# Decay and key mask accumulated by TensorE in two attentions of a two-layer kernel, and the forgetting attention one unit apart

## The reference, cut to what matters

```python
# sparse attention: of the keys of a query only the selected ones count
_, sel = lax.top_k(score, topk)
logits = jnp.einsum('bthd,btkhd->bhtk', qblk, k_sel) * scale
logits = logits - slopes * dist
p = jax.nn.softmax(jnp.where(sel_ok, logits, -inf))

# forgetting attention: a decay, cumulated over the tokens, is added to the logits
log_f = jax.nn.log_sigmoid(f_logit)
cum_f = jnp.cumsum(log_f, axis=1)
logits = jnp.einsum('bhqd,bhkd->bhqk', qb, kb) * scale
logits = logits + cum_f[..., qs:qe, None] - cum_f[..., None, :qe]
p = jax.nn.softmax(jnp.where(causal, logits, NEG_INF))

# pooling mixer: moving means of four widths, less the input, times a 64x64 matrix for each group
groups.append((cs_g - lagged) / count - uf)
y = einsum('bsgc,gcd->bsgd', p, w_pool) * pool_scale
```

## Time and profile before

| what | value |
|---|---|
| median of three runs | 3217.14 us |
| the profiled execution's own time | 3217.12 us |
| its span, first to last instruction | 3215.0 us |
| mean granted clock of TensorE, share of 2.4 GHz | 0.961 |
| busy: TensorE, VectorE, ScalarE, GpSimd | 3027.6, 1371.4, 643.4, 1456.7 us |
| chain that ended last: TensorE, VectorE, DMA, ScalarE | 86%, 4%, 3%, 2% of the span |

### The profile page before, as it was taken

The page is one execution under the profiler, slowest core; times in us unless marked ns, Lnnn a source line. Parts: engine busy times, 40 slices in busy tenths (PEclk is TensorE's granted clock), DMA queues, the critical chain, the costliest instruction groups (busy, mean ns, idle before and its releaser), DMA issues.

```text
span 3215.0 us, 33121 instructions
## 1 busy us (share of the span) xinstructions
PE 3027.6 (94%) x13405; PEld 2224.9 (69%) x13405; DVE 1371.4 (43%) x2007; ACT 643.4 (20%) x1068; POOL 1456.7 (45%) x895
## 2 busy tenths in 40 slices
PE   7999979789999999999999787999998999999997
PEld 4444446457888888887886444667666888887886
DVE  0499957646523235343307334111312532335323
ACT  1401046421100001210302443110121211121111
POOL 2000100345665657666665112335435666667663
PEclk8999989889999999999999778999999999999998
DMA  4111136132333333433432000333333233333332
GB/s 96 33 40 33 39 102 176 53 113 85 96 108 92 104 93 95 129 92 92 120 97 66 1 1 7 79 102 108 79 91 132 86 98 95 91 103 116 95 100 64
DMA packets 364920, 273.23 MB, mean 85 GB/s; under 512 B 14048, under 2 KB 334816, under 8 KB 364768
## 3 DMA queue, kind: packets, MB, share of 16 engines
q1 hardware_dynamic: 357568, 253.30, 27.6%
q10 hardware_dynamic: 4720, 10.68, 0.9%
q0 software_dynamic: 2480, 7.13, 0.7%
HBM read 262.59 MB, written 8.49 MB: 84 GB/s over the span
## 4 chain that ended last, share of the span: by engine, by line
PE 86%; DVE 4%; DMA 3%; issue 3%; ACT 2%; POOL 2%; SPq 0%; DVEq 0%; ACTq 0%; POOLq 0%
PE PS L803 38%; PE PS L815 24%; PE PS L755 5%; PE PS L769 4%; DMA ring<-in_w_in 3%; PE PS L446 3%; PE PS L459 2%; PE PS L1023 2%; PE PS L479 2%; PE PS L875 2%; PE PS L970 1%; POOL w_low L1888 1%; PE PS L471 1%; PE PS L889 1%; ACT arena L519 1%
## 5 line engine op out<-in xcount | busy, mean ns | idle before, releaser
L1888 POOL TENSOR_TENSOR w_low<-ring,w_high 128x1024 fp32r<-128x1024 f32 x382 | 940.9, 2463 | 31.9
L1885 POOL TENSOR_SCALAR w_high<-ring 128x1024 fp32r<-128x1024 f32 x382 | 427.1, 1118 | 865.9 <-PE PS L815 372.4
L815 PE MATMUL PS<-w_high,hid_high 128*128 128x512 f32 x864 | 337.2, 390 | 9.1 <-issue 9.1
L815 PE MATMUL PS<-w_high,hid_low 128*128 128x512 f32 x864 | 336.8, 390 | 0.0
L815 PE MATMUL PS<-w_low,hid_high 128*128 128x512 f32 x864 | 336.7, 390 | 0.0
L1947 POOL TENSOR_TENSOR arena<-arena 128x896 f32<-128x896 f32 (+5 forms) x24 | 39.8, 1677 | 582.0 <-DVE arena L1484 358.5
L803 PE MATMUL PS<-hT_high,w_high 128*128 128x512 f32 x656 | 272.2, 415 | 15.1 <-POOL w_low L1888 15.1
L803 PE MATMUL PS<-x1T_high,w_high 128*128 128x512 f32 x704 | 275.0, 391 | 3.5 <-DVE x1T_low L1587 3.5
L803 PE MATMUL PS<-x1T_high,w_low 128*128 128x512 f32 x704 | 274.6, 390 | 0.0
L803 PE MATMUL PS<-x1T_low,w_high 128*128 128x512 f32 x704 | 274.4, 390 | 0.0
L803 PE MATMUL PS<-hT_high,w_low 128*128 128x512 f32 x656 | 256.9, 392 | 0.0
(11 more groups left out here) (265 smaller groups left out, 4901.3 us busy)
## 6 DMA issues: line engine op xcount, KB each, us to landing
ring<-in_w_ff SPq DMA_DIRECT2D x128, 512.0 KB, 3.8
ring<-in_w_in SPq DMA_DIRECT2D x112, 512.0 KB, 3.9
ring<-in_w_gu SPq DMA_DIRECT2D x88, 512.0 KB, 3.8
ring<-in_w_ada SPq DMA_DIRECT2D x48, 512.0 KB, 5.1
ring<-in_w_down SPq DMA_DIRECT2D x44, 512.0 KB, 3.6
ring<-in_w_out SPq DMA_DIRECT2D x32, 512.0 KB, 4.5
ring<-in_w_branch SPq DMA_DIRECT2D x16, 512.0 KB, 3.9
arena<-in_x SPq DMA_DIRECT2D x8, 512.0 KB, 6.9
```

Of the source, the lines that this page charges most:

```text
L815: mm = pe.matmul(PS[:, 2 * p + half, :], x[:, k, at], w[:, q, half_of(half)], start=(first and n == 0), stop=(last and n == 2))
L1885: pool.tensor_scalar(w_high[:, q, :], ring[:, s, :], 1.0, 1.0, ALU.mult, ALU.mult).then_inc(weights_high, 1)
L1888: pool.tensor_tensor(w_low[:, q, :], ring[:, s, :], w_high[:, q, :].bitcast(F32), ALU.subtract).then_inc(weights_used[s], 1)
```

## The change

It adds an argument more to Attention: a second matmul accumulated on each score product. For the sparse attention that is a bf16 identity times the key mask, on all 128 partitions, for b of at least 2; GpSimd's adds and their buffers go. For the forgetting attention it is a selector holding -8 in the row of its head, times cum_r, which holds the cumulated decay as a rounded high part in rows 0 to 7 and 64 to 71 and the rest in rows 32 to 39 and 96 to 103, both in fp32r, K = 64 on the same half as the scores. The spreads, their copies and GpSimd's causal adds go; one causal row serves all units as bias. ScalarE makes the high parts and VectorE the low ones. All three attentions now have lag 1 written in; the forgetting one gets six buffers and the sparse one's order of units. The pool product becomes a fill of its first four units in bank 7, scaled beside them by VectorE.

```diff
-        cbias = view(141.5, 4, S)
+        ident16 = view(142, P // 2).bitcast(BF16)
...
-        selw = view(28, 8, P)
+        selw, selw_r = view(24, 8, P), rounded("selw_r", 28, 8, P)
+        cum_r = rounded("cum_r", 24, S)
+        causal_row = view(20, S)
         qk2T = view(96, 8, S)
         z2T = view(128, 8, S)
-        negcum = [view(152, 2, S), view(136, 2, S)]
-        prob2 = [view(kb, S) for kb in (160, 164, 168, 172)]
-        probT2 = [view(176, NB, 2 * P), view(20, NB, 2 * P)]
+        prob2 = [view(kb, S) for kb in (160, 164, 168, 172, 152, 156)]
+        probT2 = [view(176, NB, 2 * P), view(136, NB, 2 * P)]
...
-                return 2 * (u % (2 + self.lag)) + m
+                return 2 * (u % 3) + m
...
+                            more = self.more(pe, u, m, c, w) if self.more is not None else None
                             mm = pe.matmul(PS[:, 2 * m + c // 512, 0:w], self.q(j, m, b), self.k(j, m, c, w),
-                                           start=True, stop=True)
+                                           start=True, stop=more is None)
+                            if more is not None:
+                                mm = pe.matmul(PS[:, 2 * m + c // 512, 0:w], *more, start=False, stop=True)
...
-                for u in range(last + 1 + self.lag):
+                for u in range(last + 2):
                     if u < last:
                         scores(u + 1)
                     if self.fill is not None and u <= last:
                         self.fill(pe, u)
-                    t = u - self.lag
+                    t = u - 1
                     if t >= 1 and self.closes(t - 1):
...
-                    if u >= 2 + self.lag:
-                        dve.wait_ge(self.turned, self.turns_before[u - 1 - self.lag])
+                    if u >= 3:
+                        dve.wait_ge(self.turned, self.turns_before[u - 2])
...
-        pairs4 = [(j, b) for j in range(4) for b in reversed(range(NB))]
+        pairs4 = [(j, b) for j in range(4) for b in (6, 7, 0, 1, 4, 5, 2, 3)]
...
+            return bias8[:, 2 * j + m, P * (NB - 1 - b):S], None, 0
+
+        def c_mask(pe, u, m, c, w):
+
+            _, b = pairs2[u]
             if b < 2:
-                return bias8[:, 2 * j + m, P * (NB - 1 - b):S], None, 0
-            k = selected.index(u)
-            return cbias[:, 2 * (k % 2) + m, 0:P * (b + 1)], cbias_made, 2 * k + m + 1
+                return None
+            pe.wait_ge(ident16_made, 1)
+            return ident16, mask[b][:, c:c + w]
 
         def f_bias(u, m):
-            j, b = pairs4[u]
-            return negcum[j % 2][:, m, 0:P * (b + 1)], fbias_made, 2 * u + m + 1
+            _, b = pairs4[u]
+            return causal_row[:, P * (NB - 1 - b):S], causal_row_made, 1
+
+        def f_decay(pe, u, m, c, w):
+
+            j, _ = pairs4[u]
+            if u == 0:
+                pe.wait_ge(cum_split, 2)
+            r = slice(64 * m, 64 * m + 64)
+            return selw_r[r, 2 * j + m, :], cum_r[r, c:c + w]
...
-        SPREAD_AT = {4: (0, 0), 3: (0, 1), 2: (1, 0), 1: (1, 1)}
-
-        def spread_fill(pe, u):
-
-            j, b = pairs4[u]
-            if j == 3 or b not in SPREAD_AT:
+        def pool_fill(pe, u):
+
+            if u >= 4:
                 return
-            m, half = SPREAD_AT[b]
-            n = 4 * j + 4 - b
-            if n:
-                pe.wait_ge(negcum_made, n)
-            pe.matmul(PS[:, 7, :], selw[0:8, 2 * (j + 1) + m, :], fl[0:8, half * 512:(half + 1) * 512],
-                      start=True, stop=True).then_inc(spread_done, 1)
-
-        def spread_after(act, u):
-            j, b = pairs4[u]
-            if j == 3 or b not in SPREAD_AT:
-                return
-            m, half = SPREAD_AT[b]
-            act.wait_ge(spread_done, 4 * j + 4 - b + 1)
-            act.activation(negcum[(j + 1) % 2][:, m, half * 512:(half + 1) * 512], PS[:, 7, :], ACT.Copy, scale=-8.0
-                           ).then_inc(negcum_made, 1)
+            g, half = divmod(u, 2)
+            if u == 0:
+                pe.wait_ge(pool_w_loaded, 64)
+            else:
+                pe.wait_ge(br_bc_made, 2 + u)
+            pe.wait_ge(pooled, g + 1)
+            pe.matmul(PS[:, 7, :], pool_w[:, g, :], z2T[:, g, 512 * half:512 * half + 512], start=True, stop=True
+                      ).then_inc(pool_mixed, 1)
...
-            prob, [probT_c[:, m] for m in range(2)], (4, 5), 1, fill_c, after_c)
+            prob, [probT_c[:, m] for m in range(2)], (4, 5), fill_c, after_c, c_mask)
...
-            prob2, probT2, (4, 5), 0, spread_fill, spread_after)
+            prob2, probT2, (4, 5), pool_fill, None, f_decay)
...
-            pe.wait_ge(cum_done, 1)
-            pe.wait_ge(selw_made, 1)
-            for m in range(2):
-                p = L.pair("spread_cum", 0, m)
-                pair_here(pe, "spread_cum", 0, m)
-                for half in HALVES:
-                    mm = pe.matmul(PS[:, 2 * p + half, :], selw[0:8, m, :], fl[0:8, half_of(half)], start=True, stop=True)
-                mm.then_inc(psum_full[p], 1)
-            pe.wait_ge(pool_w_loaded, 64)
-            for g in range(2):
-                p = L.pair("pool", 0, g)
-                pe.wait_ge(pooled, g + 1)
-                pair_here(pe, "pool", 0, g)
-                for half in HALVES:
-                    mm = pe.matmul(PS[:, 2 * p + half, :], pool_w[:, g, :], z2T[:, g, half_of(half)], start=True, stop=True)
-                mm.then_inc(psum_full[p], 1)
             all_pairs_free(pe, "branch")
             forget.pe(pe)
             pe.wait_ge(forget.out_stored, forget.n_out)
-            pe.wait_ge(br_bc_made, 4)
+            pe.wait_ge(br_bc_made, 6)
...
-            act.wait_ge(br_bc_made, 2)
-            for m in range(2):
-                p = L.pair("spread_cum", 0, m)
-                unit_here(act, "spread_cum", 0, m)
-                act.activation(negcum[0][:, m, :], flat(p), ACT.Copy, scale=-8.0).then_inc(psum_free[p], 1)
-            act.wait_ge(br_bc_made, 4)
+            act.wait_ge(cum_done, 1)
+            for r in (slice(0, 8), slice(64, 72)):
+                act.copy(cum_r[r, :], fl[0:8, :]).then_inc(cum_high, 1)
             forget.act(act)
...
+            dve.wait_ge(selw_made, 5)
...
-            dve.tensor_tensor_scan(fl[0:8, :], lsf_b[0:8, :], lsf_a[0:8, :], 0.0, ALU.mult, ALU.add
-                                   ).then_inc(cum_done, 1)
+            do(dve.tensor_tensor_scan(fl[0:8, :], lsf_b[0:8, :], lsf_a[0:8, :], 0.0, ALU.mult, ALU.add))
+            dve.memset(cum_r[:, :].bitcast(F32), 0.0).then_inc(cum_done, 1)
+
+            dve.wait_ge(cum_high, 2)
+            for r in (slice(32, 40), slice(96, 104)):
+                dve.tensor_tensor(cum_r[r, :], fl[0:8, :], cum_r[0:8, :].bitcast(F32), ALU.subtract
+                                  ).then_inc(cum_split, 1)
...
-                unit_here(dve, "pool", 0, g)
-                dve.tensor_scalar(z2T[:, g, :], flat(p), pscale[:, g:g + 1], None, ALU.mult).then_inc(psum_free[p], 1)
-                freed(dve, "pool", 0, g)
-                dve.sem_inc(br_bc_made, 1)
-            forget.dve(dve, link)
+
+            def pool_out(u):
+                if u < 4:
+                    g, half = divmod(u, 2)
+                    dve.wait_ge(pool_mixed, u + 1)
+                    dve.tensor_scalar(z2T[:, g, half_of(half)], PS[:, 7, :], pscale[:, g:g + 1], None, ALU.mult
+                                      ).then_inc(br_bc_made, 1)
+
+            forget.dve(dve, link, pool_out)
...
-            for k, u in enumerate(selected):
-                j, b = pairs2[u]
-                for m in range(2):
-                    if k >= 2:
-                        pool.wait_ge(sparse.logits_made, 2 * selected[k - 2] + m + 1)
-                    pool.tensor_tensor(cbias[:, 2 * (k % 2) + m, 0:P * (b + 1)],
-                                       bias8[:, 2 * j + m, P * (NB - 1 - b):S], mask[b], ALU.add
-                                       ).then_inc(cbias_made, 1)
+            pool.tensor_copy(ident16, ident[:, :]).then_inc(ident16_made, 1)
...
-                    do(pool.memset(selw[0:8, :, :], 1.0))
-                    pool.affine_select(out=selw[0:8, :, :], in_=selw[0:8, :, :], compare_op=ALU.is_equal, fill=0.0,
-                                       base=0, pattern=[[-1, 8], [0, P]], channel_multiplier=1).then_inc(selw_made, 1)
+                    do(pool.memset(selw, -8.0))
+                    for r in (slice(32 * q, 32 * q + 32) for q in range(4)):
+                        pool.affine_select(out=selw[r], in_=selw[r], compare_op=ALU.is_equal, fill=0.0,
+                                           base=0, pattern=[[-1, 8], [0, P]], channel_multiplier=1).then_inc(selw_made, 1)
+                    pool.wait_ge(selw_made, 4)
+                    pool.tensor_copy(selw_r[:, :, :], selw).then_inc(selw_made, 1)
...
-            for u, (j, b) in enumerate(pairs4):
-                for m in range(2):
```

(11 more changed lines are left out.)

34 lines of the change are left out of this document (14 added, 20 removed).

## The result

| | before | after |
|---|---|---|
| median of 4 runs each, us | 3216.05 (3208.64 to 3218.6) | 3196.96 (3195.87 to 3201.94) |
| profiled execution, us (its span) | 3217.12 (3215.0) | 3197.6 (3195.9) |
| mean granted clock of TensorE | 0.96 | 0.97 |

The ratio of the medians is 0.9949, with a 95% interval of 0.9935 to 0.9962: 19 us less, where 23 less were forecast. The stages show where it lies. The times are VectorE's, from the start of its first logits to the end of its last store in each stage, read from the timelines of the two profiles.

The account below looks back on a forecast made before the run. No engine was taken to bound the forgetting stage, only a loop of waits per unit. Terms -38 (that stage), +10 (its start), +5 (sparse stage), 0 (selector weights) made -23 us: 3194 us, own range 3178 to 3208, 80% range 3160 to 3222.

Parts of the forecast that it names:

- the side that had 0.77: Whole kernel: faster by over 0.3%, that is below 3207.5 us, given a chance of 0.77.
- The sparse stage: Mask products and lost overlap of the heads' scores on TensorE, less relief from GpSimd's adds: +5 us, ends -10 and +26.
- I put 60% on the path: Sparse stage: of TensorE's middle extra of 26 us, 60% lengthens the stage, 15.6 us; the rest hides where VectorE was full.
- half of the 10.5: Sparse stage: VectorE's scaling loses 10.5 us of stretching by GpSimd's adds; half of that was taken off the stage.
- Rival 3: Sparse stage pays its extra whole, +26 us instead of +5, total 3215; chance 0.10.
- The start of the forgetting stage: VectorE waits for ScalarE's decay copies behind copy_v2, with pooling behind that wait: first logits at 1770.9 instead of 1761.0, 10 us lost.
- The forgetting stage: First logits to last store: four pairs of heads at 44 us plus pool products, fill and end, 187 instead of 225, gain 38.
- the sum over eight steps: Forgetting stage: one pair's eight unit steps with lag 1 add to 41 us at full clock, 44 at an assumed clock of 0.9.
- the loop through VectorE's scaling: Forgetting stage before: no engine bounds it, a chain of waits per unit does; TensorE's weight loads waited 52.9 us for VectorE's scaling.
- 1 (37 us a pair): Forgetting stage becomes as full as the differential one, 37 us a pair of heads, 28 us less in four, total 3166; chance 0.24.
- 2 (row halves one after another in the forgetting scores): Forgetting scores: head 0's decay product stops the row halves overlapping, 9.7 us more a pair, 39 in all, total 3233; chance 0.08.
- 4 (52 a pair): Forgetting stage: lag 1 gives only the sparse stage's pace, 52 us a pair, 32 more, total 3226; chance 0.06.

Follow-up runs that it names:

- experiment 1: Changed kernel with the sparse attention's key mask left out altogether, and GpSimd's copy of the 16-bit identity with it: 3167.41 us, sparse stage 104.2.
- experiment 2: Changed kernel with both heads' score products issued before both added products, for each chunk of keys: 3168.13 us, sparse stage 103.1, forgetting stage 176.2.
- Experiment 3: Changed kernel with ScalarE's two rounded decay copies ahead of copy_v2(1) and VectorE's two subtractions behind its pooling: 3179.52 us, first forgetting logits at 1771.4.
- experiment 8: Changed kernel without the decay products in the forgetting attention's scores, the decay's rows still made: 3188.51 us, forgetting stage 172.5.
- experiment 7: Changed kernel with the forgetting attention's units in the old order, 7 down to 0: 3184.23 us, forgetting stage 166.4.
- experiment 6: Changed kernel with the forgetting attention no unit apart, as before, decay still on TensorE and units in the new order: 3204.85 us, forgetting stage 203.9.
- Experiment 9: Changed kernel with the forgetting attention in the old order and no unit apart, decay still on TensorE: 3219.13 us, forgetting stage 201.6.
- experiment 11: Changed kernel with both heads' scores first in the sparse attention alone, split rows made earlier and forgetting units in the old order: median 3141.75 us, ratio 0.9773.
- experiment 4: Changed kernel with the sparse mask added to the bias on GpSimd again, the forgetting attention as changed: 3172.08 us, sparse stage 107.0.

## Why the prediction was right, and where it wasn't

The sum came to -19.1 us where -23 was forecast, inside the range and on the side that had 0.77. It is closer than its terms, and that is luck: one was 13 us too good, another 6.5 too bad, and 3.2 us came from where nothing was forecast.

**The sparse stage is the term that was mis-sized**: +5 forecast, +18.1 measured. Its parts for TensorE were near: 21.5 to 30 us forecast at full clock, of it 7.5 for the mask products and 14 for the lost overlap; by experiments 1 and 2 some 24, of it 9 and 15 (estimates above). The mechanism, heads one after another, stands in the chain. The stage grew by more than the 15 us that I had named as the sign of a wrong step. What failed are the two steps behind TensorE's work. "I put 60% on the path" was 91%, measured at two different clocks (0.75 without the mask, 0.81 with it). The reason given for 60%, that VectorE was full in nearly half of the stage, held for the kernel before only: the same edit took 12 us off VectorE, so the cover was gone just where I counted on it. That is my reading; no run has the mask on TensorE and GpSimd's adds beside it. And "half of the 10.5" of relief, with 5 more for earlier logits and a better clock, was 3.5 in all; the clock didn't rise (0.80 before, 0.81 after). The contention itself was larger than forecast, 13.5 us instead of 10.5: the 610 ns taken as the undisturbed scaling were stretched as well, and became 518. 21.6 less 3.5 is the +18.1. Rival 3, the extra paid whole, came nearer than the forecast for this stage, though its whole, 3215, didn't come true.

**The start of the forgetting stage**: 10 forecast, 10.1 measured, with every step in its place: ScalarE's copies were forecast to end at 1751.9, which with the 18.4 us from upstream (0.3 and 18.1) is 1770.3, and ended at 1770.2; the subtractions took 2.46 us for two (2.4 forecast), the pooling 16.6 (16.5). Experiment 3 shows the cause: with the copies ahead of copy_v2 and the subtractions behind the pooling the loss is gone and 9 us are won. Which of the two moves would do alone was not run.

**The forgetting stage**: -38 forecast, -44.5 measured. The pace of a pair was 44 in the forecast and 43.9 in the trace, at a granted clock of 0.88 where I took 0.9. Its two parts were less exact and made up for each other: 29 us of work at 0.9 are 32 busy us a pair and 12 of waiting, where the stage has 146.23/4 = 36.6 and 33.8/4 = 8.4, its pool products and ends included. The decay products were put at 2.05 us a pair, 8.2 for four; experiment 8 gives 7.8. What was too high is the fill and the end: 11 us beside the four pairs' 176, where 180.3 - 4 x 43.9 = 4.7 are left. But the sum over eight steps, right for this order, cannot rank two of them: by the same steps I expected the old order to take 6 to 16 us more (experiment 7), and it took 13.9 less. Two thirds of that came with a higher granted clock, which the sum took as one given number for the stage.

The reason named first, the loop through VectorE's scaling, holds but is not all. One unit apart, TensorE's weight loads wait 17.0 us for L570 instead of 55.2 (experiment 6), where the forecast had that wait gone, and this is worth 23.6 us in the new order. The other 21 us of the gain are not in any price of the forecast. Experiment 9 finds them in TensorE's busy time, 23.0 us less for about the same work, at a granted clock of 0.84 instead of 0.74. The forecast had that right as far as it goes: its spreads gone (four of 0.85 us in a pair) and its new products (2.05 in a pair, and the pool's) nearly cancel. It had the higher clock too, as the assumed 0.9, but gave it no share of its own in the 38 us and no cause. That GpSimd's additions and ScalarE's copies lay beside the loop, costed at nothing, fits as far as waits go: the time in which TensorE wasn't busy didn't change without them (experiment 9). Whether they or the spreads held the clock down stays open.

**GpSimd's selector weights**: costed at nothing, and no loss shows there. The four selections took 4.56 us from 1641.26 on, and the 10.1 us by which the stretch up to the forgetting stage grew are those of its start, above.

**The rivals.** 1 (37 us a pair): not in the changed kernel; the shortest forgetting stage (experiment 11) has a pair at 164.8/4 = 41.2 at most. 2 (row halves one after another in the forgetting scores): refuted. In the chain above the scores of both heads stand as four records in 1.06 us, and their decay products as two in 0.23, for 512 columns each, the price of one product of one pass. The Trainium skill, "TensorE: Matmul & The Clock Gate", Part 3, What overlaps and what doesn't, has matmuls start in strict program order; the trace of after disagrees, with the second head's score among the four records that come ahead of the first head's decay product, which stands before it in the program. The trace of before disagrees as well, with products on different groups of 32 rows. 4 (52 a pair): 43.9.

**The rest**, -3.2 us behind the forgetting stage, was not forecast. It is 1223.4 to 1229.2 us in the profiles here, over code that none of the edits touches; I have not followed it further.

## What to carry to other kernels

A product that is added to scores should be no higher than the scores, or stand behind both heads' scores: with full-height products between the half-height ones this stage took 125.8 us, with the same products behind them 103.1. Before a busy time of TensorE is called work that came or went, multiply it with the granted clock of its window: by that estimate 23 us that seemed to be saved work in the forgetting stage were the clock, and the mask's 9 us of work were hidden by it. When an edit frees the engine that covers its cost, price it against the profile that will be, not the one that is: cover and relief were the same microseconds of VectorE, and, as I read it, were counted twice. And ahead of any wait that a new preparation needs, look at what the engine already has queued: two small copies behind one call, and a wait for them ahead of the pooling, held back 16.6 us of work that had run for free.

## What the runs showed of the hardware

- The order of issue decides whether products on the two row halves overlap. Scores of two heads, 64 rows each, 512 columns, fp32: 1.13 us for both when adjacent (experiment 2), 1.05 to 1.12 for each when a product on all 128 rows stands between. Added products of 64 rows between them did no such harm.
- Changing between half and full height cost little beyond that: a 512-column mask product took 0.32 us in the chain between scores at full clock (572.12), beside 0.227 for one in a run of full-height products of one pass.
- The granted clock fell to 0.66 and 0.63 (a mean over the window; at the lower of its two levels, 1.2 of 2.4 GHz, it would be 0.5 throughout) in windows in which TensorE was busy for 13.48 and 10.95 of 15 us, in the sparse stage of the changed kernel. A modelled busy time does not tell which clock is granted: the stage with the scores side by side and the mask behind them, with less busy time (79.37 of 101), had 0.88 in all four profiles, and without any mask (81.36 of 104) it had 0.75.
- The forgetting stage of before was granted 0.74 and took 225 us; with the spreads, their copies and GpSimd's additions gone, the decay and pool products in their place, and the units in the same order and distance, it was granted 0.84 and took 202, for about the same work of TensorE by the estimate (experiment 9).
- The same products, in another order of units, ran at 0.93 instead of 0.88, and in three profiles of the old order one unit apart the stage stood at 0.93 to 0.95, in seven of the new order at 0.87 to 0.92. Two thirds of what the order was worth between experiment 7 and the changed kernel came in this way.
- Taking GpSimd's additions away sped up VectorE's scaling from 938 to 518 ns in the mean, 13.5 us in all, and shortened the sparse stage by 3.5, while the granted clock fell from 0.80 to 0.75 (experiment 1). With the additions back it was 938 again (experiment 4).
